# Pool corrections in one function with their products, a far norm on every second tick, and two of the last eight scalings on GpSimd

## The reference, cut to what matters

```python
x = x + 0.5 * swiglu(rmsnorm(x, ffn1_norm), w_gate, w_up, w_down)     # D_FF = 2816
h = rmsnorm(x, mix_norm)
u = h @ w_in                                                         # pool | q | k | v, 512 each
y_pool = pool_mixer(u_pool, pool_w, pool_scale) @ w_branch_pool
y_attn = chunk_attention(q, k, v, rel_bias) @ w_branch_attn          # chunk 64, 8 chunks back
gates = sigmoid(h @ w_gate + b_gate)
x = x + (gates[0] * y_pool + gates[1] * y_attn) @ w_out
x = x + 0.5 * swiglu(rmsnorm(x, ffn2_norm), w_gate2, w_up2, w_down2)
return rmsnorm(x, final_norm)
```

## Time and profile before

| | us |
|---|---|
| median of 3 runs | 1511.02 |
| profiled execution, its time | 1518.19 |
| its span, slowest core (core 6) | 1516.6 |
| spans of all cores | 1506.4 to 1516.6 |
| TensorE busy | 1488.8 (98%) |
| VectorE busy | 541.0 (36%) |
| ScalarE busy | 463.1 (31%) |
| GpSimd busy (issuing DMAs) | 66.3 (4%) |

### The profile page before, as it was taken

The page is one execution under the profiler, slowest core; times in us unless marked ns, Lnnn a source line. Parts: engine busy times, 40 slices in busy tenths (PEclk is TensorE's granted clock), DMA queues, the critical chain, the costliest instruction groups (busy, mean ns, idle before and its releaser), DMA issues.

```text
span 1516.6 us, 20636 instructions; the slowest of 8 cores (1506.4 to 1516.6 us)
## 1 busy us (share of the span) xinstructions
PE 1488.8 (98%) x7598; PEld 673.4 (44%) x7598; DVE 541.0 (36%) x872; ACT 463.1 (31%) x696; POOL 66.3 (4%) x129
## 2 busy tenths in 40 slices
PE   6999999999999999999999999999999999999997
PEld 2444444444444444444444444444444444444444
DVE  2313324112526554213335311124626555111124
ACT  3313112211357634113122311112358534111112
POOL 0000000000000000000000000000000000000000
PEclk9999999999999999999999999999999999999999
DMA  9863346998640454543364993344530643442333
GB/s 196 190 107 53 58 86 103 192 175 141 104 81 2 75 93 96 102 80 67 51 133 78 185 215 59 55 76 84 86 57 2 102 83 66 84 73 50 61 54 112
DMA packets 32482, 142.89 MB, mean 94 GB/s; under 512 B 2816, under 2 KB 5248, under 8 KB 21888
## 3 DMA queue, kind: packets, MB, share of 16 engines
q0 software_dynamic: 18000, 115.09, 45.5%
q1 hardware_dynamic: 14384, 26.48, 5.7%
HBM read 248.25 MB, written 8.39 MB: 169 GB/s over the span
## 4 chain that ended last, share of the span: by engine, by line
PE 94%; DMA 3%; DVE 1%; ACT 1%; issue 1%; DVEq 0%; SPq 0%; ACTq 0%; POOLq 0%
PE ps L400 80%; PE ps L388 5%; PE ps L878 4%; PE ps L965 2%; PE ps L927 2%; DMA xs<-xT 2%; DMA ring<-wst 1%; PE ps L456 1%; PE ps L433 0%; DVE hs L505 0%; DVE ftmp L460 0%; DVE xs L662 0%; ACT L499 0%; ACT ftmp L939 0%; DVE ps L935 0%
## 5 line engine op out<-in xcount | busy, mean ns | idle before, releaser
L400 PE MATMUL ps<-hs,ring 128*128 128x512 bf16 x3672 | 807.4, 381 | 0.6 <-DMA ring<-wst 0.6
L400 PEld LDWEIGHTS ps<-hs,ring 128*128 128x128 bf16 x3672 | 360.3, 98 | 437.6 <-issue 14.4
L400 PE MATMUL ps<-areg,ring 128*128 128x512 bf16 (+1 forms) x2004 | 436.2, 373 | 0.0
L585 DVE TENSOR_TENSOR areg<-ftmp,ps 128x512 bf16<-128x512 f32 x198 | 135.8, 688 | 524.0 <-PE ps L400 488.0
L400 PEld LDWEIGHTS ps<-areg,ring 128*128 128x128 bf16 x2004 | 196.0, 98 | 221.8 <-issue 3.8
L583 ACT ACTIVATE ftmp<-ps 128x512 f32<-128x512 f32 x198 | 118.2, 597 | 508.6 <-PE ps L400 495.7
L318 POOL DMA_DIRECT2D ring<-wst x125 | 66.1, 530 | 1390.6 <-PE ps L400 1165.9
L599 DVE SCALAR_TENSOR_TENSOR xs<-ps,xs 128x512 f32<-128x512 f32 x69 | 47.6, 690 | 165.8 <-PE ps L400 139.4
L445 ACT ACTIVATE sqt<-xs 128x512 bf16<-128x512 f32 x56 | 35.2, 629 | 216.8 <-DVE xs L599 216.8
L935 DVE TENSOR_TENSOR ps<-ps,biasT 128x512 f32<-128x512 f32 (+1 forms) x80 | 46.9, 588 | 87.5 <-PE ps L927 87.5
L505 DVE SCALAR_TENSOR_TENSOR hs<-xs,cvt,rtmp 128x512 bf16<-128x512 f32 x80 | 54.6, 746 | 36.2 <-ACT rtmp L501 36.2
(11 more groups left out here) (84 smaller groups left out, 622.6 us busy)
## 6 DMA issues: line engine op xcount, KB each, us to landing
ring<-wst POOLq DMA_DIRECT2D x81, 1024.0 KB, 10.3
ring<-wst POOLq DMA_DIRECT2D x40, 704.0 KB, 7.5
xs<-xT SPq DMA_DIRECT2D x3, 2048.0 KB, 25.3
outT<-xs SPq DMA_DIRECT2D x12, 512.0 KB, 24.5
areg<-xT SPq DMA_DIRECT2D x3, 1536.0 KB, 15.7
xs<-xT SPq DMA_DIRECT2D x8, 512.0 KB, 12.9
outT<-xs SPq DMA_DIRECT2D x8, 256.0 KB, 2.8
ring<-wst POOLq DMA_DIRECT2D x2, 512.0 KB, 9.6
```

The source lines that it names most:

```text
L400: ins = t.matmul(out_ap, l, r, start=(i == 0), stop=(i == n - 1))
L585: P.op("dve", (lambda e, bu=bu, ti=ti, j=j: e.tensor_tensor(out=a_ap(j, s), in0=ftmp[:, ti, :], in1=bank_ap(bu), op=ALU.mult)), reads=[B_t ...
```

## The change

Three parts. (1) In `pooling` the product and, in tile A, the two corrections become one function, so that they go out on one tick; tile A's 24 functions become 16. (2) In the far norm of sub-tile 1, an empty function is put behind each of the eight, and six empty ones come first in place of eight. (3) In `end_quarter`, quarter 1: blocks 2 and 3 are multiplied by their gain on ACT when block 5 of the quarter has been squared, and by the reciprocal root on GpSimd at the end; DVE keeps six of eight scalings. The stores are the same, now issued behind the pair.

```diff
                 def scale(k0):
                     for kc in (k0, k0 + 1):
+                        if q == 1 and k0 == 2:
+                            P.op("pool", (lambda e, kc=kc: e.tensor_tensor(
+                                out=xs[:, kc, t0:t0 + 256], in0=xs[:, kc, t0:t0 + 256], in1=ra, op=ALU.mult)),
+                                reads=[B_rq[q]], writes=[B_xq[kc][q]])
+                            continue
                         P.op("dve", (lambda e, kc=kc: e.scalar_tensor_tensor(
...
-                        if kc % 2:
-                            P.op("sp", dma_fn(outv[:, kc - 1:kc + 1, own0 + t0:own0 + t0 + 256],
...
+                    P.op("sp", dma_fn(outv[:, k0:k0 + 2, own0 + t0:own0 + t0 + 256], xs[:, k0:k0 + 2, t0:t0 + 256]),
+                         reads=[B_xq[k0][q], B_xq[k0 + 1][q]], dma=f"st{own0}_q{q}_{k0}")
                 put_late(qi, 2, ones_mm)
+                if q == 1 and m == slots[0][0]:
+                    for kc in (2, 3):
+                        P.op("act", (lambda e, kc=kc: e.activation(
+                            out=xs[:, kc, t0:t0 + 256], in_=xs[:, kc, t0:t0 + 256], func=AF.Copy,
+                            scale=cvt[:, C_GF + kc:C_GF + kc + 1])), reads=[B_const], writes=[B_xq[kc][q]])
                 tick()
...
-                th.append(lambda src_ap=src_ap, g=g, w=w, src_b=src_b: P.op(
-                    "dve", (lambda e: e.scalar_tensor_tensor(
+                def product(src_ap=src_ap, g=g, w=w, src_b=src_b):
+                    P.op("dve", (lambda e: e.scalar_tensor_tensor(
...
-                if mt["first_own"]:
-                    th.append(lambda src_ap=src_ap, g=g, src_b=src_b: P.op(
...
-                    th.append(lambda g=g: P.op(
...
+                    if mt["first_own"]:
+                        P.op("dve", (lambda e: e.tensor_tensor(out=tmp16[:], in0=src_ap(16, 32), in1=invct[:, g, :],
...
+                        P.op("dve", (lambda e: e.tensor_tensor(out=MX[:, g, 0:16], in0=tmp16[:], in1=up32[:, g, 16:32],
...
+                th.append(product)
             th.append(lambda: save_carry(ntok))
...
                 def queue_second():
-                    side_work.extend(far_norm(xp_ap, B_xp, 1, lambda: apply_from(xp_ap, B_xp, 1, G1),
-                                              (ftmp[:, 2, :], B_tmp[2])))
-                side_work.extend([lambda: None] * 8 + [queue_second])
+                    for th in far_norm(xp_ap, B_xp, 1, lambda: apply_from(xp_ap, B_xp, 1, G1), (ftmp[:, 2, :], B_tmp[2])):
+                        side_work.extend([th, lambda: None])
+                side_work.extend([lambda: None] * 6 + [queue_second])
```

More of the change, by code:

```diff
@@ L665, in scale @@
                             reads=[B_rq[q], B_const], writes=[B_xq[kc][q]])
-                        if kc % 2:
-                            P.op("sp", dma_fn(outv[:, kc - 1:kc + 1, own0 + t0:own0 + t0 + 256],
-                                              xs[:, kc - 1:kc + 1, t0:t0 + 256]),
-                                 reads=[B_xq[kc - 1][q], B_xq[kc][q]], dma=f"st{own0}_q{q}_{kc}")
+                    P.op("sp", dma_fn(outv[:, k0:k0 + 2, own0 + t0:own0 + t0 + 256], xs[:, k0:k0 + 2, t0:t0 + 256]),
+                         reads=[B_xq[k0][q], B_xq[k0 + 1][q]], dma=f"st{own0}_q{q}_{k0}")
                 put_late(qi, 2, ones_mm)
+                if q == 1 and m == slots[0][0]:
[3 more added lines that the diff above has]
+                            scale=cvt[:, C_GF + kc:C_GF + kc + 1])), reads=[B_const], writes=[B_xq[kc][q]])
                 tick()
@@ L827, in pooling @@
                     st *= 2
-                th.append(lambda src_ap=src_ap, g=g, w=w, src_b=src_b: P.op(
-                    "dve", (lambda e: e.scalar_tensor_tensor(
+                def product(src_ap=src_ap, g=g, w=w, src_b=src_b):
+                    P.op("dve", (lambda e: e.scalar_tensor_tensor(
                         out=MX[:, g, 0:ntok], in0=src_ap(16, L), scalar=1.0 / w, in1=up32[:, g, 16:L],
                         op0=ALU.mult, op1=ALU.subtract)),
-                    reads=src_b + [B_up[g][0], B_up[g][1]], writes=[B_mx[g]]))
-                if mt["first_own"]:
-                    th.append(lambda src_ap=src_ap, g=g, src_b=src_b: P.op(
-                        "dve", (lambda e: e.tensor_tensor(out=tmp16[:], in0=src_ap(16, 32), in1=invct[:, g, :],
-                                                          op=ALU.mult)),
-                        reads=src_b + [B_cc], writes=[B_t16]))
-                    th.append(lambda g=g: P.op(
-                        "dve", (lambda e: e.tensor_tensor(out=MX[:, g, 0:16], in0=tmp16[:], in1=up32[:, g, 16:32],
-                                                          op=ALU.subtract)),
-                        reads=[B_t16, B_up[g][0]], writes=[B_mx[g]]))
+                        reads=src_b + [B_up[g][0], B_up[g][1]], writes=[B_mx[g]])
+                    if mt["first_own"]:
+                        P.op("dve", (lambda e: e.tensor_tensor(out=tmp16[:], in0=src_ap(16, 32), in1=invct[:, g, :],
+                                                               op=ALU.mult)),
+                             reads=src_b + [B_cc], writes=[B_t16])
+                        P.op("dve", (lambda e: e.tensor_tensor(out=MX[:, g, 0:16], in0=tmp16[:], in1=up32[:, g, 16:32],
+                                                               op=ALU.subtract)),
+                             reads=[B_t16, B_up[g][0]], writes=[B_mx[g]])
+                th.append(product)
             th.append(lambda: save_carry(ntok))
```

## The result

The changed kernel takes 1516.23 us (median of nine runs) against 1511.02 us: ratio 1.0032, interval [1.0023, 1.0041], so 5.2 us slower where 1.2 us were forecast. It lies above the range (1514.4). On another chip, where the kernel before took 1513.20 us, the ratio is 1.0032 again, [1.0020, 1.0045].

What follows compares the result with a forecast made beforehand. TensorE, busy 98%, was taken as the bound, so only its waits and the end count. Terms -1.67 + 3.39 + 0 + 0.30 - 0.79 = +1.2 us gave a median of 1512.3 us, range 1509.8 to 1514.4.

Steps and rivals of the forecast that it cites:

- What bounds the kernel: Whole kernel: TensorE is busy 98%, so only its waits or the time after its last matmul can change.
- Part 2, the stall: Second FFN, tile A, tick 27: ones-matmul waits 3.4 us for a square held behind eight VectorE scalings; net +1.7 us.
- the two old stalls: TensorE waits near 793 and 814 us, caused by the far norm; the new places remove both, -1.67 us.
- Part 2, the step that failed: Tick 27: the new wait priced at its length, 3.39 us; a clock fall behind it given chance 0.07.
- rival (c): Clock falls behind the 3.4 us wait at tick 27, matmuls near half pace: +4.5 us, 1516.8 us; chance 0.07.
- Part 1: Start of attention, tile A: joined corrections leave TensorE's wait for third scores unchanged; 0, at most -0.13 us.
- Part 3, the copies on ScalarE: Kernel's end: two ACT copies ahead of quarter 0's Ln delay its scalings and the last L635, +0.30 us.
- Part 3, GpSimd: Kernel's end: GpSimd's two scalings take 0.82 us each beside VectorE's six, and just fit in 1.65 us.
- rival (a): Kernel's end: GpSimd and VectorE scalings take turns, 4.0 us against 3.2, so +0.8 us, 1513.9 us; chance 0.20.
- Part 3, the gain of 0.79 us: Kernel's end: six VectorE scalings in place of eight behind the last Exp bring the last store forward 0.79 us.
- (b): Far norm's burst of scalings is hidden: old losses go, no new wait comes, 1508.9 us; chance 0.12.
- (d): Kernel's end: GpSimd's first arithmetic has a start-up cost, its pair takes 3.7 us, 1514.4 us; chance 0.06.

Runs made afterwards that it cites:

- e4: Kernel before with only the far norm's new places, its eight scalings issued in pairs on four ticks; ratio 0.9988.
- e7: Kernel before with only the far norm's new places, twelve scalings at once (first four issued again); not timed, TensorE waits 6.04 us.
- e3: Kernel before with only the joined corrections in `pooling`; ratio 0.9996.
- e8: Kernel before with only the changed end, GpSimd's two multiplications left out; not timed against the kernel before, six scalings take 2.46 us.
- e12: Kernel before with pairs of scalings on ticks 26 to 29, joined corrections, root in PSUM, ScalarE copies behind the tick, GpSimd's store third; ratio 0.9984.
- e1: Kernel before with only the far norm's new places, eight scalings at once; 1515.99 us against 1513.14, ratio 1.0021.
- e11: The changed kernel itself measured again, against the kernel before on another chip; ratio 1.0032.
- e5: Kernel before with only the far norm's new places, scalings in pairs on ticks 26 to 29, behind L599; 1509.98 us against 1512.18, ratio 0.9984.
- e14: Kernel before with eight more tiny activations on ScalarE at the start; not timed against it, the end takes 6.78 us.
- e13: Kernel before with eight more tiny memsets on VectorE during the first loads; ratio 0.9997.
- e9: Kernel before with only the changed end, last root also written to PSUM for VectorE; not timed against it, six scalings take 2.44 us.

## Why the prediction was wrong, point by point

**What bounds the kernel:** right. TensorE's waits and the last microseconds are all that moved.

**Part 2, the stall:** right in mechanism, place and size. Tick 24, the order on ScalarE and VectorE, the wait of 3.39 us, the two old stalls gone, all as worked out; e4 to e7 show that the wait goes with the number of scalings ahead of L599, by 0.66 us each.

**Part 2, the step that failed:** the sum took the wait's own length as its whole price. "It decides from a wait between 1 and 3.7 us, so 3.4 is near the end of it" was followed by a chance of 0.07, on the ground that TensorE had been busy for 60 us. That past did not protect it: seven of eight cores fell. The result is the time of the slowest of eight, so one fallen core is enough, and a chance for one core isn't the chance for the kernel. How much of the worst fall gets into the time is not shown: in the profiled execution the slowest core, 2, had lost 1.68 us, and core 4, which had lost 2.65, ended 1.1 us ahead of it. The price of rival (c) was too high, 4.5 us from a cold start where 0 to 2.65 us came; that its time of 1516.8 us lies near the result is luck: a smaller fall, a worse end than forecast and the slowest core's share came together.

**Part 1:** right, nothing. e3 has the wait of 0.71 us with another releaser.

**Part 3, the copies on ScalarE:** right in kind, too small. The longer of L644's waits, the one on the closing chain, is 1.5 us where it was 1.1 (+0.44 in the timelines, against +0.30): the two copies take 0.40 us each on the queue, and not the 0.32 of a square.

**Part 3, GpSimd:** wrong, but not by the price of its ops. They took 0.72 and 0.89 us, right in the middle, but the other assumption, that VectorE runs on beside them, failed, and rival (a), with the Trainium skill's rule beside it, was put at 0.20. Its form was other than the rival had it: in sum milder, 3.49 us and not 4.0, but VectorE was held right at the start, so that even the first store was 1.03 us late, and the stores followed in a row from 1.98 us on.

**Part 3, the gain of 0.79 us:** wrong even without GpSimd. The last store's issue was taken for the end. e8 and e12 issue it 0.6 to 0.8 us earlier, and the end comes at most 0.1 us earlier, since the DMAs of four stores are what takes the time. Row 1513.05 of the earlier trace rows was read and the 3.3 us behind it were not.

**Unforeseen: the instruction fetch**, 1.1 us in favour of the changed kernel. The prediction had no term for it.

The sum again on the typical core, from measured terms: norm's wait 3.39 - 1.67 = +1.72; clock +1.68; L635 +0.44; from the first of the last scalings to the end, medians of eight cores, the stores held +0.95 (e1's 5.81 us to 6.76), the fetch -1.12 (6.93 to 5.81): 3.67 us, against 3.45 measured on the chip of e11. It grows to 4.7 us there by the slowest of eight cores and the 0.3 us around the span, which stays open, as does the half microsecond between that and the first chip's 5.2. Rivals (b) and (d) did not come: the burst was not hidden, and GpSimd's first op had no start-up.

## What to carry to other kernels

A block of eight scalings put on a queue at once holds whatever is queued behind it for the whole block; count the instructions ahead of the next one that the bottleneck waits for, and place the block behind it (e5's ratio is 0.9984, e1's, with the block ahead, 1.0021; the fetch is out of the end in both). A wait on TensorE costs its length, and at the 2.07 us and more of these runs also a stretch at half clock on some cores or all; the slowest of eight decides. At the end of a kernel look first at whether the stores' DMAs or their issue set the time, and before a share of VectorE's two-input work is handed to GpSimd, see whether one input can come from PSUM (six scalings in 2.44 us here, and not 3.49). An edit can also move an instruction fetch into or out of the end of a kernel (here one wait less was enough), and that was worth 1.1 us, two thirds of what the placing itself gains.

## What was not expected of the hardware

The fall from full clock behind a single wait of 2.07 to 3.39 us in a stream of matmuls of 60 us and more, on some cores and not on others in the same execution. An instruction fetch of VectorE's stream, whose place depends on how many instructions stand before it, goes with a last store that lands about 1 us later: eight memsets in the first microseconds moved it (end 6.93 to 5.83 us, medians of eight cores; 6.78 in e14, on e13's chip). And GpSimd at 128x256 took 0.72 us for its first multiplication and 0.89 for its second beside VectorE (0.72 and 0.71 in e9, where the two don't hold each other); there was no start-up cost for the first arithmetic in the kernel.
